# Four attention steps instead of two in each turn beside the first two scan groups

## The reference

```python
# delta rule, both directions, 8 heads of 64: a scan over the tokens
def step(s, inp):
    r_t, w_t, k_t, v_t, kk_t, b_t = inp
    sa = jnp.einsum('bhvk,bhk->bhv', s, -kk_t)
    s = s * w_t[:, :, None, :] + sa[..., None] * b_t[:, :, None, :] + v_t[..., None] * k_t[:, :, None, :]
    return s, jnp.einsum('bhvk,bhk->bhv', s, r_t)

# differential attention of the latent tokens, 4 heads, keys of latent and context
s = jnp.concatenate([jnp.einsum('bhmqd,bhmkd->bhmqk', qr, kr),
                     jnp.einsum('bhmqd,bhmkd->bhmqk', qp, kc)], axis=-1) * scale
p = jax.nn.softmax(s.astype(jnp.float32), axis=-1)
w = p[:, :, 0] - lam * p[:, :, 1]
o = jnp.einsum('bhqk,bhkd->bhqd', w.astype(v.dtype), v)
# rmsnorm of o over each head; then [delta rule, attention] @ w_out
```

## Time and profile before

| | us |
|---|---|
| median of 3 runs | 3406.18 |
| lowest and highest | 3405.66 and 3418.04 |
| the profiled execution, its own time | 3412.58 |
| its span, first to last instruction | 3410.8 |
| mean granted TensorE clock | 0.953 |
| PE busy | 3126.0 (92%) |
| DVE busy | 2083.0 (61%) |
| ACT busy | 1424.3 (42%) |

### The profile page before, as it was taken

One profiled execution on the slowest core, in us unless ns is written; L12 is line 12 of the kernel. 1 busy time (PEld: TensorE's weight loads), 2 busy tenths in 40 slices (PEclk: granted clock), 3 DMA queues, 4 the chain that ended last, 5 costly groups with the idle time before them and its releaser, 6 DMA issues.

```text
span 3410.8 us, 53769 instructions
## 1 busy us (share of the span) xinstructions
PE 3126.0 (92%) x22240; PEld 2709.2 (79%) x22240; DVE 2083.0 (61%) x2938; ACT 1424.3 (42%) x2019; POOL 289.7 (8%) x334
## 2 busy tenths in 40 slices
PE   8999999998999999899997788888999889996898
PEld 8987887897987788798775677777888767785796
DVE  5876645687876654667556667644333467585555
ACT  5455444445445544454554323323232344313444
POOL 2000000000000000000201122111000001042000
PEclk9999999999999999999998889878999999987999
DMA  9865545786966555497640000012332233400554
GB/s 262 283 191 161 169 149 170 225 268 217 275 222 178 143 176 161 159 272 246 212 143 30 2 9 3 3 51 70 95 96 95 67 87 87 136 1 21 147 179 142
DMA packets 457693, 477.58 MB, mean 140 GB/s; under 512 B 18560, under 2 KB 348480, under 8 KB 457472
## 3 DMA queue, kind: packets, MB, share of 16 engines
q1 hardware_dynamic: 435968, 398.71, 39.2%
q0 software_dynamic: 21504, 75.72, 6.7%
HBM read 473.31 MB, written 1.05 MB: 139 GB/s over the span
## 4 chain that ended last, share of the span: by engine, by line
PE 74%; DVE 15%; ACT 6%; issue 4%; DMA 1%; POOL 0%; DVEq 0%; SPq 0%; ACTq 0%; POOLq 0%
PE banks L319 20%; PE banks L321 20%; PE banks L320 20%; DVE weights_lo L305 2%; ACT weights_hi L297 1%; PE banks L4830 1%; PE banks L4055 1%; PE banks L3919 1%; DVE arena L4476 1%; PE banks L1352 1%; DVE third_weights_split L305 1%; DVE arena L1498 1%; PE banks L4149 1%; PE banks L4801 1%; DVE first_input_split L1363 1%
## 5 line engine op out<-in xcount | busy, mean ns | idle before, releaser
L305 DVE TENSOR_TENSOR weights_lo<-raw_weights,weights_hi 128x1024 fp32r<-128x1024 f32 (+3 forms) x436 | 515.0, 1183 | 384.4 <-ACT weights_hi L297 351.1
L297 ACT ACTIVATE weights_hi<-raw_weights 128x1024 fp32r<-128x1024 f32 (+3 forms) x436 | 445.0, 1023 | 585.1 <-PE banks L321 555.2
L270 DVE TENSOR_TENSOR weights_lo<-raw_weights,weights_hi 128x1024 fp32r<-128x1024 f32 x152 | 186.6, 1229 | 372.4 <-ACT weights_hi L263 184.6
L319 PE MATMUL banks<-first_input_split,weights_hi 128*128 128x256 f32 (+1 forms) x1204 | 344.6, 286 | 11.2 <-DVE weights_lo L305 4.2
L321 PE MATMUL banks<-first_input_split,weights_lo 128*128 128x256 f32 (+1 forms) x1204 | 342.3, 284 | 0.0
L320 PE MATMUL banks<-first_input_split,weights_hi 128*128 128x256 f32 (+1 forms) x1204 | 340.2, 283 | 0.0
L263 ACT ACTIVATE weights_hi<-raw_weights 128x1024 fp32r<-128x1024 f32 x152 | 160.8, 1059 | 402.5 <-PE banks L321 396.9
L305 DVE TENSOR_TENSOR third_weights_split<-raw_weights,third_weights_split 128x1024 fp32r<-128x1024 f32 (+1 forms) x192 | 229.7, 1196 | 149.4 <-ACT third_weights_split L297 127.2
L297 ACT ACTIVATE third_weights_split<-raw_weights 128x1024 fp32r<-128x1024 f32 (+1 forms) x192 | 198.6, 1035 | 234.1 <-PE banks L321 224.8
L319 PE MATMUL banks<-work_split,weights_hi 128*128 128x512 f32 (+2 forms) x792 | 275.9, 348 | 11.8 <-DVEq L2563 7.2
L320 PE MATMUL banks<-input_split,weights_hi 128*128 128x512 f32 (+2 forms) x792 | 273.6, 345 | 0.0
(11 more groups left out here) (661 smaller groups left out, 7216.6 us busy)
## 6 DMA issues: line engine op xcount, KB each, us to landing
raw_weights<-in_w_ffn_gu SPq DMA_DIRECT2D x176, 512.0 KB, 5.3
raw_weights<-in_w_in SPq DMA_DIRECT2D x144, 512.0 KB, 3.6
raw_weights<-in_mlp_w SPq DMA_DIRECT2D x128, 512.0 KB, 3.9
arena<-in_ada_w POOLq DMA_DIRECT2D x96, 512.0 KB, 5.6
raw_weights<-in_w_ffn_down SPq DMA_DIRECT2D x80, 512.0 KB, 4.3
raw_weights<-in_w_branch SPq DMA_DIRECT2D x48, 512.0 KB, 3.5
raw_weights<-in_hy_w_in SPq DMA_DIRECT2D x48, 512.0 KB, 4.2
raw_weights<-in_ssd_w_in SPq DMA_DIRECT2D x48, 512.0 KB, 3.8
```

Of the source, the lines that this page charges most:

```text
L270: last = v.tensor_tensor(self.w_lo[:, u % 2, :], self.raw[:, u, :], self.w_hi[:, u % 2, :].bitcast(F32), ALU.subtract)
L297: last = s.activation(hi, raw, ACT.Copy)
L305: last = v.tensor_tensor(lo, raw, hi.bitcast(F32), ALU.subtract)
L319: pe.matmul(out, left_hi, right_hi, start=start, stop=False)
```

## The change

The list `running` holds each of the two attention generators four times instead of twice, so that each turn calls them four times, before one call of each scan group. Nothing else of the loop is changed; `STAGGER` stays 25. In `attention_norms`, the wait of the square on ACT for the chain's earlier steps is now there for all four tiles; the wait for the ends of attention stays at the first tile.

```diff
 def attention_norms(c, m, ch, ends):
...
         @ch.block.scalar
         def _(s):
-            if t == 0:
-                s.wait_ge(ch.steps_done, ch.steps)
-                for semaphore, value in ends:
-                    s.wait_ge(semaphore, value)
+            s.wait_ge(ch.steps_done, ch.steps)
+            for semaphore, value in ends if t == 0 else ():
+                s.wait_ge(semaphore, value)
             s.activation(square[:, t, :], q[:, t, :], ACT.Square).then_inc(ch.steps_done, 1)
...
-    running = attention + attention + [scan(g, chain_ends([mixing] + attend)) for g in groups[0:2]]
+    running = 4 * attention + [scan(g, chain_ends([mixing] + attend)) for g in groups[0:2]]
```

## The result

The changed kernel takes 3434.7 us (median of 4, 3432.8 to 3435.5) where the kernel before takes 3410.6 in the same comparison: the ratio is 1.0071, interval 1.0053 to 1.0089, that is +24 us. The forecast was 3422, range 3400 to 3434, so the time lies just outside it, on the side of slower. The forecast was added to 3406.2 for the kernel before; in the comparison that kernel took 3410.6. Of the 12.7 us between 3422 and 3434.7 the base makes 4.4, and the sum the rest (+15.9 against +24). The profiled execution took 3435.0 us, its span is 3433.2; PE is busy for 3134.7 us, against 3126.0 before.

A forecast was written before the change was run, and what follows sets the result against it. It took attention beside two groups to be bound by its chain of steps, the four groups' stretch to be near PE's bound; -8.5 + 10.5 + 18.3 - 4.4 = +15.9 us gave 3422 on the median's scale, range 3400 to 3434.

The forecast's parts named there:

- Part 1: Attention stretch, rotation to gates: with fewer scan turns beside it, it shortens by 8.5 us; bounds 0 and -20.
- part 3: Stretch with all four scan groups: five more turns and another pairing of chunk parts cost +18.3 us; bounds +9 and +25.
- part 4: The end, groups 2 and 3 alone: 25 turns instead of 30 save 4.4 us; bounds -4 and -5.5.
- Rival A: Attention doesn't shrink, its own chain or a falling PE clock setting its length: +24 us, 3430; chance 0.17.
- 2, bare turns: Turns 16 to 25, groups 0 and 1 running alone: new time of +10.5 us; bounds 10 and 14.
- Rival B: Four groups' stretch: only PE's work counts, +9 there and nothing for the pairing; whole kernel +7 us, 3413; chance 0.16.
- 5, the waits: Attention norms: the added waits of the squares on ACT are hidden by scan steps and cost 0 us.
- The sum: Whole kernel: -8.5 + 10.5 + 18.3 - 4.4 = +15.9 us.
- The signs for the reader: Profile after: attention 74 to 78 us, bare turns at half PE clock, 88 to 91 us between a group's equal marks.
- I am wrong if the period shortens: Period between a group's equal marks, 86.8 us before: if shorter, the sum over pairs of chunk parts failed.
- The Trainium skill's rule that I quoted: Attention beside scans: regimes bound by different engines may gain from interleaving; the change does the opposite, so slower.

The follow-up runs named there:

- four_136: The changed kernel with the delta rule's outputs of tiles 2, 3 and 1 held until turn 136: 3417.7 us, ratio 1.0027 to the kernel before.
- two_waits: The kernel before with only the three added waits of the squares on ACT, attention at two steps a turn: 3406.2 us, ratio 0.9998.
- two_fill: The kernel before with 36 useless matmuls in the end stretch where only groups 2 and 3 run: 3405.0 us, ratio 0.9986.
- four_late: The changed kernel with the delta rule's outputs of tiles 2, 3 and 1 held until turn 150: 3432.7 us, ratio 1.0076 to the kernel before.
- distance 20: The changed kernel with STAGGER 20 instead of 25: 3426.6 us, ratio 1.0047 to the kernel before.

## Why the prediction was wrong, step by step

Two steps failed. Part 1 sized what attention would save at more than twice what it did. And part 3 had the mechanism wrong: it charged 18.3 us to five more turns in another pairing of chunk parts. With the -4.4 of part 4 that is +13.9, where the runs show 1 to 6 us; the kernel lost most of what it lost there, 13.6 us, in one closing at half clock, which no part of the sum and no rival had.

*1, attention, -8.5:* it gave -3.6. The four blocks gave 2.7 and not 4.6: a block alone was put at 12 us from a few lines' busy time; it is 13.3, so that only 10.7 of the 64.0 us were the scans' and not 16. One step of the chain is missing in that sum, the copy on ACT, of 1.2 us a block, about the difference:

```profile
L3246 ACT ACTIVATE arena<-banks 128x512 f32<-128x512 f32 x8 | 4.8, 597 | 10.7 <-PE banks L3238 10.6
```

The rotation gave 0.5 and not 2.5 (15.0 us; alone 13.0), the gates 0.4 and not 1.4. Rival A named this cause, attention's own chain; more than half of the saving didn't come. That A's sum of +24 is the measured number is luck: it has nothing saved here and the 18.3 of the pairing.

*2, bare turns, +10.5:* it gave +8.9 by the marks. The granted clock in it was 1.00, where the prediction looked for half.

*3 and 4, four groups and the end, 18.3 - 4.4 = +13.9:* in sum it gave 17.9, near enough to look right, and for the wrong reason: luck again. Without the slow closing (four_136) it is 1 to 6 us. The error was to read the cost of a pair of chunk parts from windows and carry it to another pairing. PE's share of 78% beside an opening was not a loss that stays. Rival B, by which only PE's work counts, had +4.6 for the two parts, and with the measured parts 1 and 2 that makes +10, where four_136 took +9. That PE does later what it can't do beside an opening is B's reading and fits; no run shows it by itself.

*What no part and no rival had:* one closing at half clock, 13.6 us between four_136 and the changed kernel. I had the row for its price at hand, the last closing of the kernel before, where PE is full and the clock half, and took it for something of the end alone. Rival A even named a falling clock, but in the attention stretch, where it went from 0.79 to 0.73 over the blocks; what that cost was not taken apart.

*5, the waits, 0:* right as far as two_waits can tell, in the kernel before.

*The sum* +15.9 against +24. By the traces the terms are -3.6 + 8.9 + 0.9 (parts 3 and 4 without the slow closing, four_136) + 17.0 (from there to the changed kernel) = +23.2. *The signs for the reader:* 74 to 78 us for attention, missed by 1.7; half clock in the bare turns, missed; 88 to 91 us between equal marks, measured 84.9, 88.3 and 104.7, so only the middle one. "I am wrong if the period shortens" was not the sign that failed me, but one period of three being out of line.

The Trainium skill's rule that I quoted from "Perfetto Trace Analysis", section "Optimization Strategy", on interleaving regimes, had the sign: 15 turns of levels cost 3.6 us beside attention, and bare, 10 of them took 11.1. The Trainium skill's rule in "TensorE: Matmul & The Clock Gate", section "What's actually happening", that activity releases the clock, is not borne out in the closings if activity is read from the busy rows: in 27.6 us with PE busy throughout (STAGGER 15) the clock stayed at half, and here the measurement decides.

## What to carry to other kernels

When the order of independent chains is changed, look in the trace for stretches in which PE is fully busy at half clock before costing the pairing: here the same instructions took 1.8 times as long there, and the same closing fell into that state or not by what ran ahead of it (two_fill, four_136). Two remedies worked once each here: the work that fills DVE moved behind such a stretch instead of ahead of it (15 us), and useless matmuls in the gaps ahead of it and at its start, with which the clock stayed at full (5 us). Neither is a rule: moved to another place (four_late) the same work brought nothing, and what sets a slow closing off is not known. And a chain's length without its neighbours is worth one run: guessed from busy times a block was 10% short.

## What the runs showed of the hardware

The granted clock can stay at 0.50 while PE has no gap by the records: 9.6 us in the changed kernel (PE 9.60 of 9.60), 27.6 us with STAGGER 15 (27.60 of 27.60). Eight instructions of 128x64 fp32 products take 1.97 us there and 1.10 at full clock. The last closing took 19.1 us at a granted clock of 0.58 (at full when it began at 2247.7 us, at half from 2250.6 on) and 13.2 us at 1.00. What differed ahead of it were the 36 extra matmuls, 72 instructions of the trace: in the levels before it PE was busy for 11.82 of 12.8 us instead of 8.96 of 13.3. The same instructions in the same pairing, one chunk apart, ran at 0.72 and at 1.00 (36.0 and 25.8 us, distance 20).
